# A block with two mixers and three expert layers: groups of four modulation units moved to lie within one pass of the first mixer

## The reference

```python
mod = jax.nn.silu(c) @ w_mod[i] + b_mod[i]          # 1024 -> 6 * 1024, also for c_ctx
h_lat = modulate(x_lat, norm1_g[i], sh1, sc1)       # rms norm, scale, shift
q, v, zf, zb, g = jnp.split(h @ w_in, 5, axis=-1)   # 8 heads of 128
lf, kf = _gate(zfc, lbf); o_cf, s_f = _gla_scan(qc, kf, vc, lf, s0)   # context, forward
lf, kf = _gate(zfl, lbf); o_lf, _ = _gla_scan(ql, kf, vl, lf, s_f)    # latents, forward
# the same backward (zb, reversed), then o_lf + rev(o_lb), norm, gate with silu(g), w_out
...
mod = (silu(c_2) @ ada_w_2[i] + ada_b_2[i])         # second part: i = 0, 1, each 1024 -> 6 * 1024
```

## Time and profile before

| what | value |
|---|---|
| median of 3 runs | 2980.42 us (2976.72 to 2987.3) |
| the profiled execution | 2986.83 us, span 2985.1 us |
| granted TensorE clock, mean | 0.861 |
| TensorE busy | 2181.5 us (73%) |
| TensorE weight loads | 1541.8 us (52%) |
| VectorE busy | 1101.6 us (37%) |
| ScalarE busy | 816.1 us (27%) |
| GpSimd busy | 270.0 us (9%) |
| DMA | 698.39 MB, mean 234 GB/s |

### The profile page before, as it was taken

How to read it: one execution, slowest core, us unless ns; L and a number is a source line. 1 busy time by engine, 2 the same in 40 slices (tenths; PEclk the granted TensorE clock), 3 DMA queues, 4 the chain that set the end, 5 groups by cost and what they waited for, 6 DMA issues and landing times. The chain is left out here.

```text
span 2985.1 us, 41692 instructions
## 1 busy us (share of the span) xinstructions
PE 2181.5 (73%) x17466; PEld 1541.8 (52%) x17466; DVE 1101.6 (37%) x1660; ACT 816.1 (27%) x1333; POOL 270.0 (9%) x268
## 2 busy tenths in 40 slices
PE   5978787779799479867666653899997767676552
PEld 4856565579577268833233221677775733233221
DVE  3266656654422254441011103566545431011103
ACT  4155555532122242321000002433323311000001
POOL 2021111110110100010000001011111010000001
PEclk8988888889799789888788775999998888888776
DMA  8355555424598323279999996211111489999995
GB/s 317 98 169 177 164 176 166 159 44 147 212 318 326 131 97 99 96 312 412 392 419 413 404 398 244 64 51 44 44 44 40 192 330 410 415 402 415 407 413 198
DMA packets 218831, 698.39 MB, mean 234 GB/s; under 512 B 24365, under 2 KB 123382, under 8 KB 161782
## 3 DMA queue, kind: packets, MB, share of 16 engines
q1 hardware_dynamic: 195446, 625.04, 55.5%
q0 software_dynamic: 12992, 33.10, 3.2%
q10 hardware_dynamic: 10176, 37.23, 3.1%
HBM read 664.34 MB, written 45.11 MB: 238 GB/s over the span
## 5 line engine op out<-in xcount | busy, mean ns | idle before, releaser
L220 PE MATMUL PS<-ring,arena 128*32 128x256 f32 (+5 forms) x7584 | 816.8, 499 | 508.7 <-DMA ring<-in_moe_w_up 185.4
L220 PEld LDWEIGHTS PS<-ring,arena 128*32 128x32 f32 (+3 forms) x7584 | 423.3, 141 | 854.1 <-issue 698.8
L220 PE MATMUL PS<-second 128*128 128x256 f32 (+1 forms) x4416 | 793.4, 339 | 31.0 <-DVE second L239 28.9
L220 PEld LDWEIGHTS PS<-second 128*128 128x128 f32 x4416 | 671.6, 194 | 141.3 <-issue 26.6
L232 ACT ACTIVATE arena<-PS 128x512 f32<-128x512 f32 (+1 forms) x314 | 155.7, 496 | 1104.2 <-PE PS L220 940.3
L239 DVE TENSOR_TENSOR arena<-arena,PS 128x256 f32<-128x256 f32 (+1 forms) x83 | 43.5, 524 | 766.4 <-PE PS L220 766.1
L220 PE MATMUL PS<-arena 128*64 128x64 f32 (+8 forms) x1504 | 281.0, 369 | 26.9 <-DVE arena L250 10.6
L232 ACT ACTIVATE arena<-arena 128x512 f32<-128x512 f32 (+6 forms) x271 | 195.9, 723 | 298.2 <-DVE arena L239 150.2
L258 DVE COPY arena<-PS 128x512 f32<-128x512 f32 (+4 forms) x169 | 93.6, 554 | 421.3 <-PE PS L220 351.4
L228 PE MATMUL PS<-ident,arena 128*128 128x128 f32 x919 | 143.9, 307 | 140.5 <-ACT arena L232 90.4
L220 PEld LDWEIGHTS PS<-arena 128*128 128x128 f32 (+5 forms) x1504 | 174.7, 190 | 134.6 <-issue 105.9
(11 more groups left out here) (157 smaller groups left out, 1120.1 us busy)
## 6 DMA issues: line engine op xcount, KB each, us to landing
ring<-in_moe_w_gate SPq DMA_DIRECT2D x148, 1024.0 KB, 10.4
ring<-in_moe_w_up SPq DMA_DIRECT2D x148, 1024.0 KB, 13.0
ring<-in_moe_w_down SPq DMA_DIRECT2D x148, 1024.0 KB, 11.2
ring<-in_ada_w SPq DMA_DIRECT2D x48, 1024.0 KB, 5.3
y_d<-arena ACTq DMA_DIRECT2D x51, 512.0 KB, 8.3
ring<-in_w_mod SPq DMA_DIRECT2D x24, 1024.0 KB, 6.4
ring<-in_gdn_in_w SPq DMA_DIRECT2D x32, 512.0 KB, 4.1
ring<-in_hg_w_in SPq DMA_DIRECT2D x24, 512.0 KB, 6.8
```

The lines of the kernel that those rows point to most:

```text
L220: return P.e.matmul(o, l, r, start=st, stop=sp)
```

## The change

Units 14 and 15 move ahead of the passes, to 12 and 13. The passes 0 to 13 then hold four units each, 16 to 71, and passes 14 and 15 none; before, passes 0 to 13 held 14 to 69, and pass 14 the last two. So a group of four now begins at the first place of a pass and ends at its fourth; before, it began at the third place of one pass and ended at the second of the next. With it ScalarE's copy goes from the second place to the fourth, and the turn and VectorE's addition from the third to the first of the next pass. The places themselves stay.

```diff
     MODS_OF = [[] for _ in range(16)]
-    for n in range(14, 72):
-        MODS_OF[(n - 14) // 4].append(n)
+    for n in range(16, 72):
+        MODS_OF[(n - 16) // 4].append(n)
@@ hgrn_sp
-        for n in (12, 13):
+        for n in range(12, 16):
             mod_sp(n, turn)
@@ hgrn_pe
-        mods_pe((12, 13))
+        mods_pe(range(12, 16))
@@ hgrn_ve
-        mods_ve((12, 13))
+        mods_ve(range(12, 16))
```

## The result

The changed kernel is **slower by 0.28%**: median 2993.32 us of 14 runs against 2985.40 of 14 runs of the kernel before beside them, ratio 1.0028 with a 95% interval of 1.0018 to 1.0038. The forecast was 2985 us, that is 4.8 us above the three-run median of 2980.42; the measured difference of the medians is 7.9. Of the 8.3 us between 2985 and 2993.3, 5.0 lie in the start: the kernel before has a median of 2985.40 over fourteen runs. The profiled execution has a span of 2991.4 us, 6.3 above the one of before.

The account below looks back on a forecast made before the run. A pass was bound by a ScalarE, VectorE and GpSimd chain plus the way from state update to next chain, not by TensorE. +10.8 - 3.8 - 2.3 + 0.1 = +4.8 us on 2980.42 gave 2985 us, range 2974 to 2997.

Parts of the forecast that it names:

- seven even passes (0 to 12): State update to next chain: ScalarE's copy queues evictions and a table load behind the fourth unit; +1.5 us each, +10.8.
- six odd passes (1 to 11): Copy hides under VectorE's work; modulation addition moves to the next pass, `o` is added earlier: -0.64 us each, -3.8.
- pass 13: No high or low parts left, so VectorE waited for `o`; copy done at about 578.6 against squares at 580.93: -2.3 us.
- pass 0, up to its state update: Units 14 and 15 fit TensorE's idle time ahead; their copy delays ScalarE once by 0.5 against busy VectorE: +0.1 us.
- term for the clock: `o` and `q` on TensorE in even passes: loss from its slow clock, taken as 1.6 us between 0 and 3.2.
- Part 3: Odd passes: copy done 5.1 us after the state update, up to 7, hidden under VectorE; -3.8 us in six passes.
- Part 4: Other moves: VectorE's modulation addition, ahead of `kd`'s eviction, hidden, without cover 0.3 us; units ahead of pass 0, +0.1.
- A: Rival: slow TensorE clock eats most of `o` and `q`, 3.2 us lost per even pass; +16, 2996 us; 17%.
- B: Rival: no loss of clock on TensorE, even way 14.43 us; sum -6.5, 2974 us; 9%.
- C: Rival: TensorE is the bound, `o` comes 3.8 us earlier in 14 passes; -53, 2927 us; 4%.
- D: Rival: ScalarE's table load coming onto the path costs 2.7 us instead of 1.30; +15, 2995 us; 3%.
- F: Rival: period unchanged, the moved copy finds its unit early and waits only change names; 2980 us; 7%.

Follow-up runs that it names:

- e1: Changed kernel, with ScalarE's copy moved behind the next pass's table loads and VectorE's modulation addition behind its evictions of `kd` and `sc`: 2960.35 us, ratio 0.9908.
- e5: Kernel before, own grouping, with ScalarE's copy ahead of its four exponentials instead of behind them: 2955.40 us, ratio 0.9893.
- e7: Changed kernel, with ScalarE's eviction of `o` (squares of `o` in odd passes) ahead of the copy of the fourth unit: 2988.06 us, ratio 1.0006.
- e4: Changed kernel, with 24 needless products on TensorE ahead of `o` in passes 0 to 13: 2974.42 us, ratio 0.9965.
- e2: Changed kernel, with VectorE's modulation addition moved behind the evictions of `kd` and `sc`: 2992.01 us, ratio 1.0015.
- e9: Kernel before, with ScalarE's copy ahead of its four exponentials and 24 needless TensorE products ahead of `o`, run beside e8: 2943.99 us, ratio 0.9867.
- e8: Repeat of e5 (kernel before, copy ahead of the four exponentials), on one chip with e9: 2954.24 us, ratio 0.9905.

## Why the prediction was right, and where it was off

It was right on the direction of the sum, on the range, and on the mechanism. Of the time itself it told 60%: +4.8 of +7.9 us. It called such a change "the same", taking 0.3% as what can be told; the interval of 0.1% to either side tells 0.28% from nothing. By its steps, in the profiled executions:

| step | forecast | measured |
|---|---|---|
| seven even passes (0 to 12) | +10.8 | +10.7 |
| six odd passes (1 to 11) | -3.8 | -3.3 |
| pass 13 | -2.3 | -1.4 |
| pass 0, up to its state update | +0.1 | +2.5, with 0.7 less before it |
| pass 14 and after | 0 | +1.0 up to the gate's first transposes, -2.5 behind them |

The measured column is from the table of ways: in even passes (15.75 - 14.89) + 1.16 + 2.48 + 1.23 + 1.18 + 2.54 + 1.25. It adds up to 6.3, as the spans do.

**The even passes.** The order of the queue was the right reading, and e1, e5 and e7 show it as cause: the same regrouping with the copy elsewhere is 1.2% faster than the changed kernel, and one eviction put ahead of the copy takes its own 0.6 us off. The term for the clock was 1.6 us between the ends of 0 and 3.2; against e4's ways of 14.0 it was 1.6 to 1.7 in five passes and 3.0 in the two long ones, 2.0 in the mean. That the sum came so near (1.53 us a pass against 1.5) is luck: the clock took 0.4 us more than forecast, and the way at full clock was 14.0 us, 0.4 less than the 14.43 of my terms. About half of the latter is the length of `o`, which I took from a merged row (2.03); from start to start it is 307.93 - 306.12 = 1.81 in e4. The waits for line 250 ahead of `o` were 6.9 us in odd passes as told, but only 3.1 to 4.8 in even ones, where I had put 5 to 7; this didn't enter the sum.

**The odd passes.** The way got shorter by about 0.6 us in five of the six, near the 0.64 told (passes 3, 5, 9 and 11 took 9.91 to 9.93 instead of 10.51 to 10.58, pass 1 took 10.20 instead of 10.77); pass 7 took 10.30, only 0.2 less, which stays open. VectorE is the cover there, and the copy behind the fourth unit lay under it: in pass 5 it starts at 351.01 where VectorE's addition of `o` was still to come.

```profile
351.01 0.38 ACT L232 ACTIVATE arena<-PS 128x256 f32<-128x256 f32 x1 [1.55 <-PE PS L220]
```

**Pass 13** fell short, since `o` and the last unit both ran slow there and the copy was done 6.3 us after the state update, not the 5.35 that the -2.3 rests on (Part 3's own sum for the odd passes gives 5.1). TensorE, then ScalarE:

```profile
582.52 3.76 PE L220 MATMUL PS<-arena 128*128 128x128 f32 x16 [6.92 <-DVE arena L250]
586.21 1.94 PE L220 MATMUL PS<-ring,arena 128*32 128x256 f32 x16
```

```profile
588.21 0.38 ACT L232 ACTIVATE arena<-PS 128x256 f32<-128x256 f32 x1 [4.86 <-PE PS L220]
```

**The step that failed** is the one on VectorE's addition in Part 4: "Hidden; without that cover 0.3". I had tested it at passes whose TensorE is ahead and whose clock is up. In pass 0 neither is so, and the chain took 2.0 us more; with the addition elsewhere (e2) 1.5 of them came back. The 0.7 us less ahead of the chain no run explains. The price without cover was wrong too: it isn't the addition's own 0.2 us but the whole wait for the turn, with the eviction of `kd` queued behind it. For the copy of unit 15, half a microsecond was forecast as delay of ScalarE; it is there (the next chain starts 21.47 us after the first, not 20.99), but I took it to be hidden behind VectorE.

**The rivals.** A (loss of 3.2 in every even pass) came near in two of seven, with 3.0. B (no loss of clock) is what e4 builds: 14.0 us, near the 14.43 that it was priced at. C (-53 us) fell for the reason given; but e5 shows that the wait was worth 31 us once nothing is behind the copy. D is settled by the rows of the table load: from 326.45 to the Silu at 327.74 it is 1.29 us. The 2.66 us for each switch of set in the Trainium skill ("ScalarE: Activation LUTs", What ACT_TABLE_LOAD costs) are not seen in this trace: a load costs about 1.28 us there and nothing shows behind it. F fell with the interval above 1.0018.

What is open: of the 7.9 us of the medians, 6.3 are in the two traces; the last 2331.3 us of before and 2328.8 of after, behind the gate's first transposes, differ by more than that gap, and no run here explains their scatter.

## What to carry to other kernels

A wait on the busiest engine is worth what comes late next, and the instruction that was moved to remove it brings its own wait along: list what is queued behind its new place on its engine, and what of that lay under other work. Here one copy of 0.38 us, put behind the fourth unit, carried 3 us of evictions and a table load out from under `q`; the same copy put into an idle time of its own engine gave 1.1%. And a cover has to be looked up at the first pass of a loop as well, where engines stand otherwise to each other than in the steady state.

## What the runs showed of the hardware

After waits of 3.1 to 6.9 us in passes 1 to 13 of the changed kernel, sixteen tiles of 128x128 took 3.0 to 3.76 us instead of 2.05, at a granted clock of 0.50 for at least a part of them. Behind waits of 2.5 us, in the odd passes from 3 on of e5, they took 3.3 to 3.65 us; in pass 5 the granted clock was 0.50 from 330 to 332, and the wait had ended at 329.17. Behind the 1.40 us of pass 0 of e5 they took 2.02. 24 needless products in the idle time of the changed kernel, 3.1 us of work, made two groups of needed work 1.6 to 2.9 us shorter (e4), and they made the kernel with the better place for the copy 10 us faster (e9 against e8). The mean granted clock of the profiled executions was 0.870 in e8 and 0.875 in e9. Useless work pays here in a stage where TensorE is no bound, because `o` and `q` lie on the way from one pass to the next.
